# Norming the first eight heads while the last pair is computed, and starting the output projection with half sums of four tiles

## The chip, the cores and the metric

The kernel is one program on one core of a Trainium2 chip. Its engines are TensorE (PE: matrix products and transposes; "PEld" in a profile is its weight load), VectorE (DVE), ScalarE (ACT), GpSimd (POOL) and SyncE (SP, which here only issues transfers). Each engine works through its own list of instructions in order; semaphores order work between engines. The metric is the device time of one execution in microseconds; less is better.

## The reference, cut to what matters

Two transformer blocks run one after the other on 256 tokens of width 1024. The change lies in the second block, between its attention and the projection behind it. The sixteen heads are computed, the first eight (neighbourhood attention) and the last eight (dilated attention) are each normed over their own 512 features, and the two halves side by side go through one 1024 x 1024 projection:

```python
y = jnp.concatenate([rmsnorm(merge(o_na), out_norm_na_g[l]),
                     rmsnorm(merge(o_dil), out_norm_dil_g[l])], axis=-1) @ w_out[l]
x = x + g1 * y
h2 = rmsnorm(x, norm2_g[l]) * (1.0 + sc2) + sh2
```

`rmsnorm` divides by the root of the mean square over the features and multiplies by a gain. What comes behind (`h2`, its queries and the two large tables) is not touched.

## The kernel before

Activations are kept transposed: a tile is 128 features x 256 tokens. Sixteen heads are eight pairs, one tile `oT[:, n, :]` a pair; tiles 0 to 3 are the first eight heads, tiles 4 to 7 the last eight. Every float32 product is made of three fp32r products: each operand is split into a high part (`WH`, `YH`, written by ScalarE) and a low part (`WL`, `YL`, the difference, written by VectorE), and TensorE adds high x high, high x low and low x high. A tile of the output projection thus is 8 x 3 = 24 matmuls of 128x256, and its eight tiles are 192.

Weights come as a stream of chunks of 128x1024, one chunk an output tile, through a ring of four slots (`raw`, `WH`, `WL`). `hi(c)` on ScalarE makes the high part of chunk `c` once the tile of chunk `c - 4` is done (`chunk_done`); `lo(c)` on VectorE makes the low part once the high one is there (`h_done`), and TensorE waits for it (`l_done`). The chunks of the output projection are `C_COUT` to `C_COUT + 7`. Before the change the attention's steps prepare them up to `C_COUT + 2`; `C_COUT + 3` is prepared as the first thing of the projection's loop.

The attention is software-pipelined over steps m = 0 to 10 (`mix_step` on three engines). A step m < 8 projects the queries and keys of pair m; TensorE then computes the scores of pair m - 1 (L1608), the values product of pair m - 2 (`values`, L1630), the transposes of the probabilities of pair m - 1 (`turn_probs`, L1620) and of the output of pair m - 2 (`turn_out`, L1638). VectorE adds the bias and takes the maximum (`soft_in`: L971, L976, L982), divides the output by its sum (`o_out`, L1005, tile `on`) and, a step later, copies the transposed output to `oT` (L1107, semaphore `ot_done`). ScalarE computes the exponentials (`exps`, L510), copies the transposed probabilities (`pt_out`, tile `pT`, L520) and squares the `oT` tiles (L475); GpSimd adds the squares (L1411). So the last pair has its scores in step 8, its values in step 9, and its `oT` tile in step 10.

A norm is `spread(k)` on TensorE (a product with ones that sums the squares over partitions, L1530), then `rms(k)` on VectorE: the mean into `nm` (L808), a wait for `root(k)` on ScalarE (square root of `nm` into `nt`, L403), the reciprocal (L810) and one Newton step (L800 to L803) into `R`. Norm 4 is that of the first eight heads, norm 5 that of the last eight. Behind them `normed` multiplies `oT` by gain and `R` into `FY` (L1134, semaphore `yf_ready`), `norm_high` on ScalarE makes `YH` (L615) and `normed_low` on VectorE makes `YL` (L867, `yl_ready`). The order on VectorE behind the steps is written out:

```python
steps(dve, mix_step)
rms(4, D // 2, EPS_B, ps[:, 0, T:2 * T])
...
normed(0)
rms(5, D // 2, EPS_B, ps[:, 7, 0:T])
normed(1)
normed_low(0)
normed_low(1)
```

TensorE's projection, `out_steps`, waits once for all eight `YL` tiles and then does the eight output tiles one after the other in two alternating banks (L1495). VectorE adds each, scaled, to `x` (`cout_step`, L1150); ScalarE squares the new `x` for the next norm.

Of the kernel before, what the change touches and what calls it, by code (L numbers as in the profile page):

```python
# [16 lines left out]
T = 256  # L17
# [89 lines left out]
def two_block_kernel(nc, stream, xT, vecs, cI, cB, rows, wsT, adaT, att_bias, skT, spill, out):  # L107
    with ExitStack() as ctx:
# [267 lines left out]
        def _(act):  # L376
# [215 lines left out]
            def mix_step(m, g=None):  # L592
                if m < 8:
                    hi(C_QK + 2 * m + 3, g)
                    act.wait_ge(chunk_done, up(C_QK + 2 * m + 1, g, 4))
                    act.wait_ge(s_mm, up(8 + m - 1, g, 2))
                    act.activation(qs[:, m % 2, :], ps[:, m % 2, 0:T], ACT.Copy).then_inc(qt_ready, 1)
                    hi(C_QK + 2 * m + 4, g)
                if g is not None or m >= 3:
                    sq_tile(24 + m - 3, oT, ot_done, m - 2, m - 3, g, 2)  # L600
                if 1 <= m <= 8:
                    exps(8 + m - 1, g, False)
                if m < 8:
                    load_ada(41 + m, g)
                if 1 <= m <= 8:
                    pt_out(8 + m - 1, g)
                    if m < 8:
                        load_bias(m + 1, g)
# [8 lines left out]
            root(4)  # L617
# [7 lines left out]
            def cout_step(n, g=None):  # L625
                hi(C_COUT + 3 + n, g)
                if g is not None or n >= 1:
                    cout_square(n - 1, g)
# [147 lines left out]
        def _(dve):  # L776
# [324 lines left out]

            def mix_step(m, g=None):
                if m < 8:
                    lo(C_QK + 2 * m + 3, g)
                if g is not None or m >= 3:
                    dve.wait_ge(ot_mm, up(8 + m - 2, g, 2))
                    dve.tensor_copy(tiles(oT, m - 3, g, 2), ps[:, 2 + m % 2:3 + m % 2, T:2 * T]).then_inc(ot_done, 1)  # L1107
                if 1 <= m <= 8:
                    soft_in(8 + m - 1, g, False)
                if 2 <= m <= 9:  # L1110
                    o_out(8 + m - 2, g)
                if m < 8:
# [11 lines left out]
            rms(4, D // 2, EPS_B, ps[:, 0, T:2 * T])  # L1124
# [4 lines left out]
            dve.wait_ge(ot_done, NPAIR)  # L1129

            def normed(k):

                for n in range(4 * k, 4 * k + 4):
                    dve.scalar_tensor_tensor(out=FY[:, n, :], in0=oT[:, n, :], scalar=vec[:, V_OG + n:V_OG + n + 1],  # L1134
                                             in1=R[:, k, :], op0=ALU.mult, op1=ALU.mult).then_inc(yf_ready, 1)

            def normed_low(k):
                for n in range(4 * k, 4 * k + 4):
                    y_low(n, AG + 8 + n, FY[:, n:n + 1, :], None, 1)

            normed(0)
            rms(5, D // 2, EPS_B, ps[:, 7, 0:T])
            normed(1)
            normed_low(0)
            normed_low(1)

            def cout_step(n, g):
                lo(C_COUT + 3 + n, g)
                dve.wait_ge(chunk_done, up(C_COUT + n + 1, g, 4))
                dve.scalar_tensor_tensor(out=tiles(x, n, g, 4), in0=ps[:, n % 2:n % 2 + 1, 0:T],  # L1150
# [3 lines left out]
            with dve.Fori(0, 2) as g:  # L1154
                for n in range(4):
                    cout_step(n, g)

            dve.wait_ge(bias_in[0], (NPAIR // 2 + 1) * 16)
            dve.tensor_tensor(diags[:, :, :], ident.unsqueeze(1).broadcast_to([P, KC, P]),
                              mod[:, 40:48].unsqueeze(2).broadcast_to([P, KC, P]), ALU.mult).then_inc(diag_ready, 1)  # L1160

# [324 lines left out]
        def _(pe):  # L1486
# [214 lines left out]
            def mix_step(m, g=None):  # L1701
# [4 lines left out]
                if 1 <= m <= 8:  # L1706
# [4 lines left out]
                    scores(8 + p, g, p % 2)  # L1711
                if m >= 2:
# [17 lines left out]
                if m == 8:  # L1730
                    spread(4, sacc_done, 28, tmp[5][:, :], bank=0, at0=T)
# [3 lines left out]
            out_steps(C_COUT, AG + 16, 24)  # L1735
# [227 lines left out]
```

## Time and profile before

| what | us |
|---|---|
| median of 3 runs | 1441.45 (1438.92 to 1443.35) |
| the profiled execution: its time | 1439.84 |
| its span, first to last instruction | 1437.8 |
| TensorE busy | 1312.4 (91%) |
| VectorE busy | 1003.8 (70%) |
| ScalarE busy | 758.1 (53%) |
| GpSimd busy | 348.0 (24%) |
| mean granted TensorE clock | 0.956 of full |

The profile's times are microseconds from the start of the span. A granted clock of 1.00 is TensorE's upper level, 2.4 GHz, and 0.50 the lower, 1.2 GHz. A busy TensorE need not be at its peak; idle time of an engine that nothing waits for costs nothing.

### The profile page before, as it was taken

What the parts mean: (1) busy time and instruction counts of PE and PEld (TensorE: products, weight loads), DVE (VectorE), ACT (ScalarE), POOL (GpSimd) and SP (SyncE); (2) the same over time, 40 slices, a digit from 0 to 9 for tenths busy, and PEclk for the clock granted to TensorE, in tenths of its full rate; (3) what the DMA queues carried; (4) which work ended last, traced back from release to release, by engine and by line L of the source; (5) the groups of instructions that cost most, each with busy time, mean ns of one, the idle gap of its engine ahead of it and who ended that gap; (6) DMA issues with size and microseconds to landing.
All of it is one profiled execution on the core that took longest, in us unless ns stands there. A gap on an engine that the chain in (4) does not pass through costs nothing.

```text
span 1437.8 us, 26848 instructions
## 1 busy us (share of the span) xinstructions
PE 1312.4 (91%) x8582; PEld 1181.9 (82%) x8582; DVE 1003.8 (70%) x1875; ACT 758.1 (53%) x1259; POOL 348.0 (24%) x233
## 2 busy tenths in 40 slices
PE   5989998998399857999999999999999999999994
PEld 5979998887398846998999977777888888888883
DVE  7689987884647755788788855555666666666664
ACT  5444354554245534554888854444555555555553
POOL 0068812112200013778677710000000000000000
PEclk9989999997699968999999999999999999999998
DMA  7867785442246513555233345555565655655562
GB/s 287 326 226 253 260 261 165 147 149 77 100 162 216 179 45 126 163 165 188 91 107 114 118 134 179 180 179 172 181 193 183 192 188 187 191 181 192 182 194 97
DMA packets 67878, 249.18 MB, mean 173 GB/s; under 512 B 7792, under 2 KB 8176, under 8 KB 66928
## 3 DMA queue, kind: packets, MB, share of 16 engines
q1 hardware_dynamic: 59184, 216.89, 45.9%
q10 hardware_dynamic: 8640, 31.59, 6.5%
q8 instruction: 31, 0.51, 0.1%
q14 instruction: 23, 0.19, 0.0%
HBM read 245.83 MB, written 2.62 MB: 173 GB/s over the span
## 4 chain that ended last, share of the span: by engine, by line
PE 82%; DVE 10%; ACT 3%; issue 2%; DMA 1%; POOL 1%; DVEq 0%; ACTq 0%; SPq 0%; POOLq 0%
PE ps L1495 34%; PE ps L1823 25%; PE ps L1834 10%; PE ps L1836 5%; PE ps L1804 4%; ACT pr L510 2%; DVE s L971 1%; DVE small L976 1%; PE ps L1620 1%; PE ps L1608 1%; DVE R L810 1%; PE ps L1630 1%; DVE WL L785 1%; PE ps L1566 1%; DMA ada<-adaT 1%
## 5 line engine op out<-in xcount | busy, mean ns | idle before, releaser
L785 DVE TENSOR_TENSOR WL<-raw,WH 128x1024 fp32r<-128x1024 f32 x326 | 409.3, 1259 | 175.7 <-ACT WH L399 172.7
L399 ACT ACTIVATE WH<-raw 128x1024 fp32r<-128x1024 f32 x394 | 414.0, 1055 | 195.5 <-PE ps L1495 87.1
L1495 PE MATMUL ps<-X,WH 128*128 128x256 f32 x1872 | 351.9, 289 | 13.3 <-DVE X L1089 7.4
L1495 PEld LDWEIGHTS ps<-X,WH 128*128 128x128 f32 x1872 | 295.8, 195 | 15.1 <-DVE X L1089 8.2
L1495 PE MATMUL ps<-X,WL 128*128 128x256 f32 x936 | 267.4, 286 | 0.0
L1834 PE MATMUL ps<-X,WH 128*128 128x512 f32 x608 | 216.9, 397 | 0.0
L1823 PE MATMUL ps<-WH,wvH 128*128 128x512 f32 x512 | 205.6, 402 | 2.5 <-DVE wvL L1289 2.1
L1823 PE MATMUL ps<-WH,wvL 128*128 128x512 f32 x512 | 202.6, 396 | 0.0
L1823 PE MATMUL ps<-WL,wvH 128*128 128x512 f32 x512 | 202.3, 395 | 0.0
L1464 POOL TENSOR_TENSOR WL<-raw,WH 128x1024 fp32r<-128x1024 f32 x68 | 164.4, 2420 | 82.9 <-ACT WH L399 82.8
L1495 PEld LDWEIGHTS ps<-X,WL 128*128 128x128 f32 x936 | 181.6, 194 | 0.0
L1836 PE MATMUL ps<-X,WL 128*128 128x256 f32 x608 | 170.5, 280 | 0.0
L1834 PEld LDWEIGHTS ps<-X,WH 128*128 128x128 f32 x608 | 114.2, 188 | 27.6
L1823 PEld LDWEIGHTS ps<-WH,wvH 128*128 128x128 f32 x512 | 96.9, 189 | 39.4 <-DVE wvL L1289 15.6
L1836 PEld LDWEIGHTS ps<-X,WL 128*128 128x128 f32 x608 | 114.7, 189 | 2.9
L1823 PEld LDWEIGHTS ps<-WH,wvL 128*128 128x128 f32 x512 | 96.6, 189 | 22.4
L1823 PEld LDWEIGHTS ps<-WL,wvH 128*128 128x128 f32 x512 | 96.7, 189 | 17.4
L1495 PE MATMUL ps<-WH,X 128*128 128x256 f32 (+1 forms) x416 | 79.5, 292 | 24.3 <-DVE X L1089 19.4
L1495 PE MATMUL ps<-YH,WH 128*128 128x256 f32 x256 | 73.9, 289 | 17.4 <-DVE YL L867 17.4
L1495 PEld LDWEIGHTS ps<-WH,X 128*128 128x128 f32 x416 | 68.3, 201 | 25.9 <-issue 24.6
L740 ACT ACTIVATE tmp<-tmp 128x256 f32<-128x256 f32 x76 | 31.7, 418 | 107.7 <-DVE tmp L1298 107.7
L1495 PE MATMUL ps<-YL,WH 128*128 128x256 f32 x256 | 73.4, 287 | 0.0
(233 smaller groups left out, 2070.1 us busy)
## 6 DMA issues: line engine op xcount, KB each, us to landing
raw<-stream SPq DMA_DIRECT2D x394, 512.0 KB, 3.4
ada<-adaT ACTq DMA_DIRECT2D x48, 512.0 KB, 3.6
bias<-att_bias ACTq DMA_DIRECT2D x9, 512.0 KB, 4.6
x<-xT SPq DMA_DIRECT2D x1, 1024.0 KB, 4.7
ws<-wsT SPq DMA_DIRECT2D x1, 1024.0 KB, 7.1
lng<-rows SPq DMA_DIRECT2D x1, 1024.0 KB, 8.0
lnb<-rows SPq DMA_DIRECT2D x1, 1024.0 KB, 7.6
bsb<-rows SPq DMA_DIRECT2D x1, 1024.0 KB, 7.6
```

What stands on the lines that cost most here:

```text
L399: act.activation(WH[:, slot, :], raw[:, slot, :], ACT.Copy).then_inc(h_done, 1)
L510: act.activation(pr[:, k, :], s[:, k, :], ACT.Exp, bias=negm[:, k:k + 1], accum_out=small_den[:, par, k:k + 1]).then_inc(p_ready, 1)
L740: act.activation(tmp[i % 2][:, :], tmp[i % 2][:, :], ACT.Gelu).then_inc(gelu_ready, 1)
L785: dve.tensor_tensor(WL[:, slot, :], raw[:, slot, :], WH[:, slot, :].bitcast(F32), ALU.subtract).then_inc(l_done, 1)
L810: link(dve.reciprocal(R[:, k % 2, :], nt[:, :]))
L971: ins = dve.scalar_tensor_tensor(out=s[:, :, :].rearrange("p (h t) k -> p h (t k)", h=2), in0=ps[:, 4:6, :], scalar=HD ** -0.5, in1=b, op0 ...
L1464: pool.tensor_tensor(WL[:, slot, :], raw[:, slot, :], WH[:, slot, :].bitcast(F32), ALU.subtract).then_inc(l_done, 1)
L1495: mm = pe.matmul(out_ap, a(kc), b(kc), start=(first and kc == 0 and i == 0), stop=(last and kc == KC - 1 and i == 2))
L1804: mm = pe.matmul(ps[:, gate_bank(e) + half, k * P:(k + 1) * P], O1[:, n, :], (O2a, O2b[:, e % 2])[half][:, k, :], start=True, stop=True)
L1823: mm = pe.matmul(ps[:, 4 + 2 * t + h, :], a[:, j % 2, ts_], b[:, slot, hs], start=(first and i == 0), stop=(last and i == 2), skip_group_c ...
L1834: pe.matmul(ps[:, i % 2, :].rearrange("p (x t) -> p x t", x=2), wh(kc), X1[:, :, kc, :], start=(kc == 0), stop=False, skip_group_check=True)
L1836: mm = pe.matmul(ps[:, i % 2, 0:T], wl(kc), X1H[:, kc, :], start=False, stop=(kc == KC - 1), skip_group_check=True)
```

## The change

Five things are rearranged; no arithmetic is changed.

- Norm 4 moves into the steps. TensorE's `spread(4)` stands ahead of the values product of step 8, VectorE writes `nm` in step 8 behind `o_out`, ScalarE takes the root in step 8 between the exponentials and the copies of the transposed probabilities, and VectorE does the reciprocal, the Newton step and the first two `normed` tiles in step 9, one ahead of and one behind `o_out`.
- `hi` and `lo` of chunk `C_COUT + 3` move into step 8, at its start.
- Behind the steps VectorE does the other two tiles of the first half and their four `YL`, then norm 5, then `normed` and `normed_low` of the second half interleaved.
- TensorE takes four output tiles in four banks at once: for each the 12 matmuls of the first half of the features, and then for each the 12 of the second half. It waits for `YL` tile by tile. The last four output tiles are done as before, in the same four banks.
- The small sums on `mod` move behind the norm, and `diags` moves ahead of the last four `cout_step`.

```diff
@@ ScalarE
                     act.activation(qs[:, m % 2, :], ps[:, m % 2, 0:T], ACT.Copy).then_inc(qt_ready, 1)
                     hi(C_QK + 2 * m + 4, g)
+                if m == 8:
+                    hi(C_COUT + 3)
                 if g is not None or m >= 3:
                     sq_tile(24 + m - 3, oT, ot_done, m - 2, m - 3, g, 2)
                 if 1 <= m <= 8:
                     exps(8 + m - 1, g, False)
+                if m == 8:
+                    root(4)
...
-            root(4)
             norm_high(0)
             root(5)
             norm_high(1)
...
             def cout_step(n, g=None):
-                hi(C_COUT + 3 + n, g)
                 if g is not None or n >= 1:
+                    hi(C_COUT + 3 + n, g)
                     cout_square(n - 1, g)
@@ VectorE
+            def normed(n):
+
+                dve.scalar_tensor_tensor(out=FY[:, n, :], in0=oT[:, n, :], scalar=vec[:, V_OG + n:V_OG + n + 1],
+                                         in1=R[:, n // 4, :], op0=ALU.mult, op1=ALU.mult).then_inc(yf_ready, 1)
+
+            def normed_low(n):
+                y_low(n, AG + 8 + n, FY[:, n:n + 1, :], None, 1)
+
             def mix_step(m, g=None):
                 if m < 8:
                     lo(C_QK + 2 * m + 3, g)
+                if m == 8:
+                    lo(C_COUT + 3)
                 if g is not None or m >= 3:
                     dve.wait_ge(ot_mm, up(8 + m - 2, g, 2))
                     dve.tensor_copy(tiles(oT, m - 3, g, 2), ps[:, 2 + m % 2:3 + m % 2, T:2 * T]).then_inc(ot_done, 1)
                 if 1 <= m <= 8:
                     soft_in(8 + m - 1, g, False)
+                if m == 9:
+                    dve.wait_ge(root_ready, 5)
+                    link(dve.reciprocal(R[:, 0, :], nt[:, :]))
+                    newton(R[:, 0, :], nm[:, :], nt[:, :], r_ready)
+                    dve.wait_ge(r_ready, 5)
+                    dve.wait_ge(ot_done, 4)
+                    normed(0)
                 if 2 <= m <= 9:
                     o_out(8 + m - 2, g)
+                if m == 8:
+                    dve.wait_ge(psn_ready, 5)
+                    dve.tensor_scalar(nm[:, :], ps[:, 0, T:2 * T], 2.0 / D, EPS_B, ALU.mult, ALU.add).then_inc(m_ready, 1)
+                if m == 9:
+                    normed(1)
...
             steps(dve, mix_step)
-            rms(4, D // 2, EPS_B, ps[:, 0, T:2 * T])
+            normed(2)
+            normed(3)
+            for n in range(4):
+                normed_low(n)
+            rms(5, D // 2, EPS_B, ps[:, 7, 0:T])
+            dve.wait_ge(ot_done, NPAIR)
+            for n in range(4, 8):
+                normed(n)
+                if n >= 5:
+                    normed_low(n - 1)
+            normed_low(7)
...
-                dve.scalar_tensor_tensor(out=tiles(x, n, g, 4), in0=ps[:, n % 2:n % 2 + 1, 0:T],
+                dve.scalar_tensor_tensor(out=tiles(x, n, g, 4), in0=ps[:, n:n + 1, 0:T],
@@ TensorE
                     scores(8 + p, g, p % 2)
+                if m == 8:
+                    spread(4, sacc_done, 28, tmp[5][:, :], bank=0, at0=T)
...
-                if m == 8:
-                    spread(4, sacc_done, 28, tmp[5][:, :], bank=0, at0=T)
 
             steps(pe, mix_step)
             spread(5, sacc_done, 32, qb[:, 0, :])
-            out_steps(C_COUT, AG + 16, 24)
+
+            def cout_half(n, k0):
+
+                pe.wait_ge(l_done, C_COUT + n + 1)
+                wh, wl = weight(WH, (C_COUT + n) % RING), weight(WL, (C_COUT + n) % RING)
+                for kc in range(k0, k0 + 4):
+                    if n == 0:
+                        pe.wait_ge(yl_ready, AG + 8 + kc + 1)
+                    yh, yl = YH[:, kc, :], YL[:, kc, :]
+                    for i, (a, b) in enumerate(((wh, yh), (wh, yl), (wl, yh))):
+                        mm = pe.matmul(ps[:, n, 0:T], a(kc), b, start=(kc == 0 and i == 0), stop=(kc == KC - 1 and i == 2))
+                return mm
+
+            pe.wait_ge(m_ready, 5)
+            for n in range(4):
+                if n == 2:
+                    pe.wait_ge(ot_done, NPAIR)
+                cout_half(n, 0)
+            for n in range(4):
+                cout_half(n, 4).then_inc(chunk_done, 1)
+            with pe.Fori(1, 2) as g:
+                for n in range(4):
+                    pe.wait_ge(x_ready, up(20 + n + 1, g, 4))
+                    feature_tile(C_COUT + n, g, n, YH, YL)
             spread(6, sacc_done, 40, tmp[5][:, :])
```

What the program's lists of instructions show of this, at three places. First VectorE from the start of step 8 (behind the steps' loop), before; the first five rows are step 8:

```order
L1107 COPY oT<-ps 128x256
L971 SCALAR_TENSOR_TENSOR s<-ps,bias 128x1024
L976 TENSOR_REDUCE small<-s 128x4
L982 TENSOR_SCALAR small<-small 128x4
L1005 TENSOR_TENSOR on<-ps,small 128x256
L996 RECIPROCAL small<-small 128x4
L1107 COPY oT<-ps 128x256
L1005 TENSOR_TENSOR on<-ps,small 128x256
L1107 COPY oT<-ps 128x256
L808 TENSOR_SCALAR nm<-ps 128x256
L810 RECIPROCAL R<-nt 128x256
```

The same engine and place in the changed kernel (L788 is `lo`, L1120 the copy to `oT`, L974 to L985 `soft_in`):

```order
L788 TENSOR_TENSOR WL<-raw,WH 128x1024
L1120 COPY oT<-ps 128x256
L974 SCALAR_TENSOR_TENSOR s<-ps,bias 128x1024
L979 TENSOR_REDUCE small<-s 128x4
L985 TENSOR_SCALAR small<-small 128x4
L1008 TENSOR_TENSOR on<-ps,small 128x256
L1134 TENSOR_SCALAR nm<-ps 128x256
L999 RECIPROCAL small<-small 128x4
L1120 COPY oT<-ps 128x256
L1125 RECIPROCAL R<-nt 128x256
L803 TENSOR_TENSOR nt<-R 128x256
```

The low part of a chunk now stands ahead of the last pair's `soft_in`, and the reciprocal of norm 4 two rows behind the last exponentials' sum instead of behind the last `oT`.

Second ScalarE from step 8 on; the lines with + and - are of one piece of the difference:

```order
+L399 ACTIVATE WH<-raw 128x1024
 L475 ACTIVATE tmp<-oT 128x256
 L510 ACTIVATE pr,small<-s,small 128x256 x4
-L520 ACTIVATE pT<-ps 128x512 x2
-L475 ACTIVATE tmp<-oT 128x256 x2
 L403 ACT_TABLE_LOAD
 L403 ACTIVATE nt<-nm 128x256
-L615 ACTIVATE YH<-FY 128x256 x4
+L520 ACTIVATE pT<-ps 128x512 x2
+L475 ACTIVATE tmp<-oT 128x256 x2
+L619 ACTIVATE YH<-FY 128x256 x4
```

The high part of the chunk stands ahead of the square and the exponentials, and the one table load and the square root ahead of the copies to `pT`.

Third TensorE behind the steps' loop, before and then in the changed kernel (L1550 is `spread`, L1628 the scores, L1650 the values, L1640 and L1658 the transposes):

```order
L1608 MATMUL ps<-ks,qs 128x256 x4
L1630 MATMUL ps<-vC,pT 128x64 x8
L1620 MATMUL ps<-idio,pr 128x128 x8
L1638 MATMUL ps<-idio,on 128x128 x2
L1530 MATMUL ps<-tmp,ones 128x256
L1630 MATMUL ps<-vC,pT 128x64 x8
L1638 MATMUL ps<-idio,on 128x128 x2
L1530 MATMUL ps<-qb,ones 128x256
```

```order
L1550 MATMUL ps<-tmp,ones 128x256
L1650 MATMUL ps<-vC,pT 128x64 x8
L1640 MATMUL ps<-idio,pr 128x128 x8
L1658 MATMUL ps<-idio,on 128x128 x2
L1650 MATMUL ps<-vC,pT 128x64 x8
L1658 MATMUL ps<-idio,on 128x128 x2
L1550 MATMUL ps<-qb,ones 128x256
```

`spread(4)`, the product on `tmp`, moved from behind the last pair's transposes to ahead of the values of the pair before it; behind `spread(5)` the projection starts in both.

## Rows read from the trace of the kernel before

**Rows 1.** Waits of TensorE, 490 to 580 us: total, times, longest.

```profile
PE ps L1495 <- DVE YL L867: 14.4, 1, 14.4
PE ps L1495 <- DVE X L1089: 7.4, 1, 7.4
```

**Rows 2.** Chain that ended last, in order of time: start, us, what.

```profile
508.83 0.43 DVE oT L1107
...
524.82 1.10 DVE YL L867 x3
...
526.25 24.47 PE ps L1495 x192
```

**Rows 3.** Timeline of VectorE, 487 to 522 us: start, us, instruction, idle before.

```profile
487.04 1.23 DVE L785 TENSOR_TENSOR WL<-raw,WH 128x1024 fp32r<-128x1024 f32 x1 [1.44 <-ACT WH L399]
488.18 0.42 DVE L1107 COPY oT<-ps 128x256 f32 x1
...
496.53 1.23 DVE L971 SCALAR_TENSOR_TENSOR s<-ps,bias 128x1024 f32<-128x1024 f32 x1 [0.17 <-PE ps L1608]
...
507.62 0.42 DVE L1005 TENSOR_TENSOR on<-ps,small 128x256 f32<-128x256 f32 x1 [4.06 <-PE ps L1630]
...
511.46 1.75 DVE L810 RECIPROCAL R<-nt 128x256 f32<-128x256 f32 x1 [1.88 <-ACT nt L403]
...
514.49 0.43 DVE L803 TENSOR_TENSOR R<-R,nt 128x256 f32<-128x256 f32 x1
...
517.16 0.42 DVE L808 TENSOR_SCALAR nm<-ps 128x256 f32<-128x256 f32 x1
...
521.56 1.67 DVE L1134 SCALAR_TENSOR_TENSOR FY<-oT,vec,R 128x256 f32<-128x256 f32 x4
```

**Rows 4.** Timeline of ScalarE, 485 to 524 us.

```profile
485.47 0.59 ACT L520 ACTIVATE pT<-ps 128x512 f32<-128x512 f32 x1
485.94 1.06 ACT L399 ACTIVATE WH<-raw 128x1024 fp32r<-128x1024 f32 x1
...
495.71 0.59 ACT L520 ACTIVATE pT<-ps 128x512 f32<-128x512 f32 x1
...
501.14 0.19 ACT L510 ACTIVATION_READ_ACCUMULATOR pr<-s,small 128x1 f32 x1
502.71 1.09 ACT L520 ACTIVATE pT<-ps 128x512 f32<-128x512 f32 x2 [1.38 <-PE ps L1620]
...
509.72 1.28 ACT L403 ACT_TABLE_LOAD   x1
511.01 0.42 ACT L403 ACTIVATE nt<-nm 128x256 f32<-128x256 f32 x1
...
522.07 1.60 ACT L615 ACTIVATE YH<-FY 128x256 fp32r<-128x256 f32 x4 [4.05 <-DVE FY L1134]
```

**Rows 5.** Timeline of TensorE, 501 to 530 us.

```profile
501.38 1.29 PE L1620 MATMUL ps<-idio,pr 128*128 128x128 f32 x8 [2.96 <-ACT pr L510]
...
503.94 3.65 PE L1630 MATMUL ps<-vC,pT 128*128 128x64 f32 x16
...
510.64 1.22 PE L1530 MATMUL ps<-qb,ones 128*128 128x256 f32 x2 [1.85 <-POOL qb L1411]
526.25 0.58 PE L1495 MATMUL ps<-YH,WH 128*128 128x256 f32 x1 [14.39 <-DVE YL L867]
...
529.40 0.31 PE L1495 MATMUL ps<-YH,WL 128*128 128x256 f32 x1
```

**Rows 6.** Windows: us, busy us of each engine (instructions), PEclk, DMA share, GB/s.

```profile
499.00:500.00 1.00, 0.00 (x0) 0.00 (x0) 0.61 (x3) 0.75 (x3) 0.00 (x0) 1.00 0.12 49
...
504.00:505.00 1.00, 1.00 (x5) 1.00 (x6) 0.00 (x0) 0.10 (x1) 0.72 (x1) 0.50 0.00 0
```

**Rows 7.** Timeline of TensorE, first block's attention: transposes of probabilities and output.

```profile
332.05 1.97 PE L1620 MATMUL ps<-idio,pr 128*128 128x128 f32 x8 [1.69 <-ACT pr L510]
333.81 0.63 PE L1638 MATMUL ps<-idio,on 128*128 128x128 f32 x2
```

More of the change, by code:

```diff
@@ L1128, in _, with cout_step @@
             link(dve.tensor_tensor(s2, s2, vec[:, V_N2:V_N2 + 8], ALU.mult))
[L1129 to L1148, printed above, removed]
+            def cout_step(n, g=None):
+                if g is not None or n >= 1:
+                    lo(C_COUT + 3 + n, g)
                 dve.wait_ge(chunk_done, up(C_COUT + n + 1, g, 4))
-                dve.scalar_tensor_tensor(out=tiles(x, n, g, 4), in0=ps[:, n % 2:n % 2 + 1, 0:T],
+                dve.scalar_tensor_tensor(out=tiles(x, n, g, 4), in0=ps[:, n:n + 1, 0:T],
                                          scalar=column(mod[:, 16:24], n, g, 4), in1=tiles(x, n, g, 4),
                                          op0=ALU.mult, op1=ALU.add).then_inc(x_ready, 1)
-            with dve.Fori(0, 2) as g:
-                for n in range(4):
-                    cout_step(n, g)
+            for n in range(4):
+                cout_step(n)
             dve.wait_ge(bias_in[0], (NPAIR // 2 + 1) * 16)
@@ L1160, in _ @@
                               mod[:, 40:48].unsqueeze(2).broadcast_to([P, KC, P]), ALU.mult).then_inc(diag_ready, 1)
+            with dve.Fori(1, 2) as g:
+                for n in range(4):
+                    cout_step(n, g)
             rms(6, D, EPS_B, ps[:, 7, 0:T])
@@ L1729, in mix_step @@
                     turn_out(8 + m - 2, g)
-                if m == 8:
-                    spread(4, sacc_done, 28, tmp[5][:, :], bank=0, at0=T)
             steps(pe, mix_step)
             spread(5, sacc_done, 32, qb[:, 0, :])
-            out_steps(C_COUT, AG + 16, 24)
+            def cout_half(n, k0):
[13 more added lines that the diff above has]
+                cout_half(n, 0)
+            for n in range(4):
+                cout_half(n, 4).then_inc(chunk_done, 1)
+            with pe.Fori(1, 2) as g:
+                for n in range(4):
+                    pe.wait_ge(x_ready, up(20 + n + 1, g, 4))
+                    feature_tile(C_COUT + n, g, n, YH, YL)
             spread(6, sacc_done, 40, tmp[5][:, :])
```

## The prediction

> **What bounds the kernel now.** I read the page first: TensorE is busy 91% of the span and holds most of the chain that ended last, so time is to be won only where TensorE stands idle and something else finishes the chain. Next I asked who TensorE waits for around the changed code. One wait stands out [rows 1]: 14.4 us in front of the second block's output projection, put down to the last `YL` tile. The 7.4 us wait behind the projection, for `X`, is not touched by the change. The chain in order of time [rows 2] shows what fills the first wait. The last pair's output is copied to `oT` at 508.83, and the projection's 192 matmuls start at 526.25, 17.42 us later, and take 24.47 us, to 550.72. Between them lie, in sequence on VectorE and ScalarE, two complete norms and sixteen split tiles. Four of the eight pairs were there long before. So the question is what part of the 17.42 us still lies between the last `oT` and the first matmul, and whether what is moved ahead of that `oT` makes it late.
>
> The timelines of VectorE, ScalarE and TensorE [rows 3 to 5] give the durations and, between two starts, the pitch. I write the new times on the scale of the old span; up to 496 us nothing differs.
>
> **Step 8: the chunk moved ahead of the last softmax.** Before, `soft_in` of the last pair starts at 496.53, as soon as its scores are there (idle 0.17, put down to TensorE) [rows 3]. Now `lo(C_COUT + 3)` is queued ahead of it on VectorE, and needs `hi(C_COUT + 3)`, which ScalarE can start only behind the copies to `pT`. The second of them starts at 495.71, and the pitch from such a copy to `WH` is 485.94 - 485.47 = 0.47 [rows 4], so `hi` runs from 496.18 to 497.24. `lo` follows 0.04 later, as 487.04 follows 485.94 + 1.06 [rows 3, 4]; the copy to `oT` follows 1.14 behind (488.18 - 487.04), at 498.42, and `soft_in` some 0.38 behind that (a copy lasts 0.42), at 498.80. The last softmax is **2.27 us late**. Queued behind the waiting `lo` are that `oT` copy, `soft_in` and `o_out`, and TensorE waits for all of them; there is no cover. The moved `hi` itself is covered: ScalarE would have been waiting for the exponentials' input.
>
> **Step 8: the root ahead of the probabilities' copies.** The exponentials ended at 501.33 [rows 4], now at 503.60, and TensorE's transposes start 2.27 later, at 503.65. They took 1.29, partly at the upper clock. In the window from 499 to 500 TensorE was idle at a granted clock of 1.00, and from 504 to 505 it had 0.50 [rows 6]. The idle stretch ahead of the transposes was 2.96 us [rows 5] and grows to about 4.7, so I take all eight at the lower level: 1.97, as the same eight in the first block at 332.05 [rows 7]. They end at 505.62. Meanwhile ScalarE does the table load and the root, 1.28 + 0.42, to 505.30 [rows 4]: hidden behind the transposes, with 0.3 us to spare. Copies to `pT` run from 505.66 to 506.75 (1.09), and the last values product starts at 506.80 against 503.94. It takes 3.65, as before [rows 5], to 510.45. `spread(4)` is gone from in front of it, but it had been hidden behind the copies (502.71 + 1.09 = 503.80), which is worth 0.1. At its new place it is free as well: TensorE then has nothing to do before the late transposes.
>
> **Step 9: the reciprocal ahead of `o_out`.** The output transposes of the pair before start some 0.2 ahead of 505.62 and take 0.63 [rows 7], to 506.04. VectorE copies `oT` at 506.08, starts the reciprocal at 506.42, and has `R` 3.46 later (511.46 to 514.49 + 0.43) [rows 3], at 509.88; `normed(0)` runs to about 510.34. `o_out` is wanted at 510.47: no delay, but only 0.1 us to spare. From `o_out` to the `oT` copy it is 1.21 (507.62 to 508.83), so the last `oT` comes at 511.68 in place of 508.83. **In all it is 2.85 us late.**
>
> **From the last `oT` to the projection.** Square, add and `spread(5)` stay: it started 1.81 behind `oT` (508.83 to 510.64) and took 1.22 [rows 3, 5]; now 513.49 to 514.71. In that time VectorE does `normed(2)` and `normed(3)`, at a pitch of 0.40 (1.67 for four, less overlap), until 512.8. ScalarE has the square to 512.6 and makes `YH` at a pitch of 0.40 (four in 1.60 [rows 4]), and VectorE's `YL` follows each: the first is there at 513.4, the fourth at 514.6. So TensorE can start right behind `spread(5)`, at **514.75 in place of 526.25**. The 17.42 us between have become 3.07.
>
> **The second half while the first runs.** Norm 5 starts at 514.75; from its `nm` to `normed` it was 4.40 (517.16 to 521.56) [rows 3], so `normed(4)` starts at 519.15, and with the interleaved order `YL` 4 is there at 520.5 and `YL` 7 at about 522.4 (eight instructions of 0.40, the first `YL` 0.1 behind its `YH`). TensorE has 48 matmuls before it needs them. Before, the first fourteen took from 526.25 to 529.40, 0.225 each, at the lower clock, and the other 178 the remaining 21.32, 0.12 each [rows 2, 5]. With that profile the 48 last 3.15 + 34 x 0.12 = 7.2, to 522.0, and the quarter of `YL` 7 is wanted at 523.0. No stall, 0.6 us to spare.
>
> **Weights behind it.** The output tile of a first chunk now ends at 523.4, behind 36 matmuls of other tiles that the old order had later; only then can `hi(C_COUT + 4)` start, and `lo` ends 1.06 + 1.23 [rows 3, 4] later, at 525.7. TensorE wants it at 514.75 + 96 matmuls, 527.7. The next chunks follow at 1.43 a tile of second halves against 2.9 us a tile of use, so the margin of 2.0 us grows. `diags` (one 128x1024 instruction, 1.23 by the nearest row, `lo`) lies in that margin. The small sums on `mod` lie behind the last `YL`, and their first user is later. The 192 matmuls so run through in 24.47 us, to 539.22 against 550.72, and behind that nothing changes its order.
>
> **The sum.** -17.42 + 3.07 + 2.85 = **-11.5 us**. Against the profiled execution, 1439.84, that is 1428.3; the median of three is 1.6 higher and scatters over 4.4, and on its scale it is 1430.0. I say 1429.5, nearer to the median.
>
> **The unknown costs and their bounds.** The late softmax is between 0 (if `lo` costs no wait) and 2.3. The matmuls at the lower clock are between none of the first fourteen (14 x 0.105 = 1.5 less) and all 48 of the first halves (34 x 0.105 = 3.6 more). I take the same fourteen, as TensorE again comes from little work (7 us after the last big product). The table load between two kinds of work was seen only behind a square, where it took 1.28; a second one's length on top is the upper bound. Together: 1429.5 - 1.5 - 2.3 = 1425.7 and 1429.5 + 3.6 + 0.9 = 1434.0.
>
> **Rivals.**
> - *The table load costs more where it stands now.* ScalarE's root is ready at 505.30 for copies at 505.66. If the load holds ScalarE for another 1.28, the root ends at 506.58, the copies are 0.93 late, and so is all behind them: -10.6, 1430.4. Against it: in the old place the root started at 511.01, the moment the load ended [rows 4]. Chance 0.06. The Trainium skill (ScalarE: Activation LUTs, "What ACT_TABLE_LOAD costs") gives about 1.28 us for the load and about 1.38 us for a drain, 2.66 in all for each switch of set; the trace agrees with the load and shows no drain behind it, though there the engine had just one instruction ahead of the load. By the page the sum would be about 1 us less gain.
> - *The first halves stay slow, or stall.* All 48 at the lower clock end at about 525.6: 3.6 us of the gain gone, 1433.1. For it: TensorE had half the clock all the way through the values product, though busy 3.65 us [rows 5, 6]. Against it: the same kind of matmul got the full clock 3.15 us after the start [rows 5]. Chance 0.10.
> - *The gain is larger*, 1426 to 1427: full clock with the first matmuls, or a softmax less late. The bound rows speak against it. Chance 0.04.
> - *The change doesn't do what it says.* The wait only moves: TensorE starts early but stands before the second halves or the fifth tile until VectorE and ScalarE have done what they did before. For it speak margins of 0.6 and 2.0 us; against it, that even a stall of 2 us leaves 9.5. To fall within 4.3 us of no change it has to lose 7.2 of the 11.5. Chance 0.04.
> - *Slower.* One mechanism does it: the granted clock. If the projection, with its new stops for `YL` one by one, stayed at 0.50 throughout, its other 178 matmuls would cost 0.105 more each, 18.7 us, which leaves the kernel 7.2 us slower, 1448.6 on the median's scale. It decides from 11.5 / 0.105 = 110 more slow matmuls, over half the projection. Against it: the half-speed stretch before lasted fourteen. Chance 0.03.
>
> **How the numbers follow.** The forecast of -11.5 has 0.73, the rivals 0.06, 0.10, 0.04, 0.04 and 0.03. About 0.3% (4.3 us) can be told from no change. All cases but the last two are faster by more: faster 0.93, same 0.04, slower 0.03. The range goes from 1425.5 to 1434.5, the bounds above with half a us for the scatter of the runs, and leaves out mainly the last two rivals.
>
> **What would show it.** In the changed kernel: `soft_in` of the last pair at 498.8, idle before it for `lo`, itself for `WH`; transposes at the lower clock; the root ending before the transposes do; the reciprocal ended before the values product; the last `oT` near 511.7; the projection's first matmul right behind `spread(5)`, near 514.8, no wait inside it, and 24 to 25 us from its first to its last. The prediction is wrong if the wait for `YL` inside the projection is more than 1 us, if the clock comes back later than 4 us after the start, or if the last `oT` is later than 513.

## The result and the profile after

The changed kernel took **1429.89 us** (median of 4 runs, 1429.45 to 1430.42) against 1442.01 (4 runs, 1438.92 to 1443.35): a ratio of 0.9923, 95% interval 0.9908 to 0.9937. It is 12 us (0.8%) faster; 1429.5 had been predicted, in a range of 1425.5 to 1434.5.

The waits of TensorE come first, now from 485 to 570 us; columns as in [rows 1].

```profile
PE ps L1515 <- DVE X L1092: 6.7, 1, 6.7
PE ps L1640 <- ACT pr L510: 5.3, 3, 4.8
PE ps L1550 <- POOL tmp L1431: 1.9, 1, 1.9
PE ps L1550 <- POOL qb L1431: 1.9, 1, 1.9
PE ps L1650 <- ACT pT L520: 0.8, 1, 0.8
```

The wait of 14.4 us for `YL` [rows 1] is gone. The wait for the last exponentials (`pr`) is longer, 4.8 against 2.96 [rows 5]: that is the late softmax. No row for `YL` is left, so the half sums never stood. The wait for `X` behind the projection reads 6.7 in place of 7.4, but nothing is won there: from the norm's mean to the first matmul of the queries it is 12.50 us against 12.49 (543.18 to 555.68, and 554.24 to 566.73). TensorE's own products between the two took 0.7 longer, since the granted clock was at 0.50 to 547 us, some 3 us, and in the kernel before for some 2; they end before `X` is there.

The timeline of VectorE:

```profile
488.00 1.23 DVE L788 TENSOR_TENSOR WL<-raw,WH 128x1024 fp32r<-128x1024 f32 x1 [1.44 <-ACT WH L399]
...
498.25 1.23 DVE L788 TENSOR_TENSOR WL<-raw,WH 128x1024 fp32r<-128x1024 f32 x1 [1.38 <-ACT WH L399]
499.39 0.42 DVE L1120 COPY oT<-ps 128x256 f32<-128x256 f32 x1
499.73 1.22 DVE L974 SCALAR_TENSOR_TENSOR s<-ps,bias 128x1024 f32<-128x1024 f32 x1
...
510.82 0.48 DVE L1107 SCALAR_TENSOR_TENSOR FY<-oT,vec,R 128x256 f32<-128x256 f32 x1
511.48 0.42 DVE L1008 TENSOR_TENSOR on<-ps,small 128x256 f32<-128x256 f32 x1 [0.17 <-PE ps L1650]
...
512.69 0.42 DVE L1120 COPY oT<-ps 128x256 f32<-128x256 f32 x1 [0.39 <-PE ps L1658]
...
515.79 0.42 DVE L811 TENSOR_SCALAR nm<-ps 128x256 f32<-128x256 f32 x1
...
520.20 0.88 DVE L1107 SCALAR_TENSOR_TENSOR FY<-oT,vec,R 128x256 f32<-128x256 f32 x2
521.17 0.43 DVE L870 TENSOR_TENSOR YL<-FY,YH 128x256 fp32r<-128x256 f32 x1
...
522.64 0.99 DVE L870 TENSOR_TENSOR YL<-FY,YH 128x256 fp32r<-128x256 f32 x2
...
526.07 1.23 DVE L788 TENSOR_TENSOR WL<-raw,WH 128x1024 fp32r<-128x1024 f32 x1 [0.60 <-ACT WH L399]
```

The first row answers to 487.04 in [rows 3]; everything here is 0.96 later for reasons ahead of the change, so I measure from that row on. `lo` at 498.25 waits for `WH`, and `soft_in` follows it without any idle time of its own: 11.73 behind the first row, against 9.49. `o_out` at 511.48 had to wait 0.17 for the values, so the reciprocal and `normed(0)` ahead of it came just in time.

ScalarE in step 8:

```profile
497.16 1.06 ACT L399 ACTIVATE WH<-raw 128x1024 fp32r<-128x1024 f32 x1
...
504.32 0.19 ACT L510 ACTIVATION_READ_ACCUMULATOR pr<-s,small 128x1 f32 x1
504.53 1.28 ACT L403 ACT_TABLE_LOAD   x1
505.82 0.42 ACT L403 ACTIVATE nt<-nm 128x256 f32<-128x256 f32 x1
506.57 1.08 ACT L520 ACTIVATE pT<-ps 128x512 f32<-128x512 f32 x2 [0.33 <-PE ps L1640]
```

The load starts 0.02 us behind the last exponential's read-out, the root 0.01 behind the load, and the copies to `pT` still wait 0.33 for TensorE: table load and root are hidden.

TensorE's timeline, and the chain over the same time:

```profile
504.56 1.97 PE L1640 MATMUL ps<-idio,pr 128*128 128x128 f32 x8 [4.76 <-ACT pr L510]
506.32 0.63 PE L1658 MATMUL ps<-idio,on 128*128 128x128 f32 x2
507.80 3.65 PE L1650 MATMUL ps<-vC,pT 128*128 128x64 f32 x16 [0.84 <-ACT pT L520]
...
515.77 0.41 PE L1765 MATMUL ps<-YL,WH 128*128 128x256 f32 x1
...
519.82 0.41 PE L1765 MATMUL ps<-YH,WL 128*128 128x256 f32 x1
520.03 0.33 PE L1765 MATMUL ps<-YH,WH 128*128 128x256 f32 x1
520.20 0.28 PE L1765 MATMUL ps<-YL,WH 128*128 128x256 f32 x1
```

```profile
514.54 1.22 PE ps L1550 x2
515.75 13.39 PE ps L1765 x96
529.15 11.40 PE ps L1515 x96
```

`spread(5)` and the 192 matmuls follow each other without a gap. 21 of them ran at the lower clock, to 520.03, where the kernel before had 14 [rows 5].

For comparisons I use **the changed stretch**: from the start of that first row (the first of the two `lo` in step 7, in every kernel) to the first matmul of the queries behind the projection. It was 79.69 us before and is 67.68 now, 12.01 less. Marks within it, in us from its start (the kernels below the second row are the experiments; "slow" counts the projection's matmuls at the lower clock; where the projection's first matmul begins under `spread(5)`, without a wait, the start given is that of its second):

| kernel | last `oT` | projection starts | last `x` | stretch | slow |
|---|---|---|---|---|---|
| before | 21.79 | 39.21 | 63.85 | 79.69 | 14 |
| changed | 24.69 | 27.75 | 52.58 | 67.68 | 21 |
| after_again | 24.68 | 27.75 | 52.61 | 67.71 | 22 |
| lo_late | 22.02 | 25.09 | 49.92 | 65.02 | 19 |
| no_halves | 24.68 | 35.67 | 60.68 | 75.78 | 17 |
| halves_alone | 20.63 | 35.50 | 60.19 | 75.94 | 15 |
| diags_back | 24.68 | 27.75 | 52.74 | 68.22 | 21 |
| root_late | 26.51 | 29.57 | 53.82 | 68.92 | 14 |
| root_again | 26.51 | 29.58 | 53.84 | 69.19 | 13 |
| warm | 21.10 | 23.61 | 48.32 | 63.42 | 0 |
| warm_split | 20.20 | 23.16 | 48.14 | 63.24 | 0 |
| warm_nm | 20.20 | 23.15 | 47.56 | 63.09 | 0 |

### The profile page after: what moved, and what is told of

The parts are those of the page before. It is cut to its first block, busy times and chain, and to the rows that moved or that the text cites. A ratio compares the mean times of both kernels' runs of the same rounds, so it can differ in the third digit from the quotient of the medians.

```text
span 1427.7 us, 26814 instructions
## 1 busy us (share of the span) xinstructions
PE 1315.0 (92%) x8582; PEld 1185.4 (83%) x8582; DVE 1004.6 (70%) x1875; ACT 758.1 (53%) x1259; POOL 345.8 (24%) x233
## 4 chain that ended last, share of the span: by engine, by line
PE 82%; DVE 9%; ACT 3%; issue 2%; DMA 2%; POOL 1%; DVEq 0%; ACTq 0%; SPq 0%; POOLq 0%
PE ps L1515 32%; PE ps L1866 25%; PE ps L1877 10%; PE ps L1879 5%; PE ps L1847 4%; ACT pr L510 2%; DVE small L979 1%; DVE s L974 1%; PE ps L1640 1%; DMA ada<-adaT 1%; PE ps L1765 1%; PE ps L1628 1%; PE ps L1650 1%; DVE WL L788 1%; PE ps L1586 1%
## 5 line engine op out<-in xcount | busy, mean ns | idle before, releaser
L788 DVE TENSOR_TENSOR WL<-raw,WH 128x1024 fp32r<-128x1024 f32 x326 | 409.8, 1261 | 174.2 <-ACT WH L399 171.4
L1326 DVE TENSOR_TENSOR tmp<-tmp,A 128x256 f32<-128x256 f32 x76 | 32.4, 426 | 51.9 <-ACT tmp L743 51.9
L1515 PE MATMUL ps<-YH,WH 128*128 128x256 f32 x224 | 64.4, 287 | 3.0 <-DVE YL L870 3.0
```

The source lines that it names most:

```text
L788: dve.tensor_tensor(WL[:, slot, :], raw[:, slot, :], WH[:, slot, :].bitcast(F32), ALU.subtract).then_inc(l_done, 1)
L1326: dve.tensor_tensor(tmp[2 + i % 2][:, :].unsqueeze(1), tmp[i % 2][:, :].unsqueeze(1), tiles(A, EARLY + i, g, 2), ALU.mult).then_inc(w_read ...
L1515: mm = pe.matmul(out_ap, a(kc), b(kc), start=(first and kc == 0 and i == 0), stop=(last and kc == KC - 1 and i == 2))
```

## The experiments

**after_again** is the changed kernel unaltered, beside root_again on the same chip.

> The changed kernel once more, unaltered, to see how far its total and the length of the changed stretch come back. From the start of the second-last lo of the steps to the first matmul of the queries behind the projection it took 67.68 us, and 79.69 in the kernel before. If that stretch is what the change moves and the rest only scatters: 67.7 to 68.3 here, with a total of 1428 to 1431.

Measured: stretch 67.71 against 67.68. Total 1427.39 (1425.76 to 1428.90), 2.5 us below the first set and below the 1428 to 1431 that I expected. But the kernel before, run beside it, was 2.5 lower too (1439.51 against 1442.01), so the difference of the medians is 12.12 us in both sets. The ratio is 0.9914 (0.9901 to 0.9928), which overlaps with 0.9923 (0.9908 to 0.9937). So a total can be set only against the kernel before of its own set, and even then the interval of a ratio is about 2 us wide to either side. The stretch of this kernel comes back to 0.03 us; where variants differ by less than the totals can tell, the stretch is what I read.

**lo_late** takes one suspected cost away.

```diff
@@ VectorE, mix_step
-                if m == 8:
-                    lo(C_COUT + 3)
...
                     dve.tensor_scalar(nm[:, :], ps[:, 0, T:2 * T], 2.0 / D, EPS_B, ALU.mult, ALU.add).then_inc(m_ready, 1)
+                    lo(C_COUT + 3)
```

> The changed kernel, with lo of chunk C_COUT+3 moved in step 8 from ahead of the oT copy and soft_in to behind nm; hi stays. Theory 1 (the moved chunk makes the last softmax 2.3 us late and nothing hides it): soft_in follows its scores at once, the values product starts 2.6 us earlier than in the changed kernel, the reciprocal still ends before it, and all behind moves with it: 2.6 us faster than the changed kernel, about 1427.3. Theory 2 (the reciprocal or the slow transposes would hold the chain anyway): the softmax is earlier but the last oT is not, 1429.9.

Measured: 1425.64 (1422.74 to 1426.98), ratio 0.9894 (0.9877 to 0.9910); stretch 65.02, 2.66 less than in the changed kernel. The rows of VectorE:

```profile
496.99 1.23 DVE L974 SCALAR_TENSOR_TENSOR s<-ps,bias 128x1024 f32<-128x1024 f32 x1 [0.16 <-PE ps L1627]
...
500.38 1.22 DVE L788 TENSOR_TENSOR WL<-raw,WH 128x1024 fp32r<-128x1024 f32 x1
```

`soft_in` waits for its scores again and not for the chunk, and `lo` lies in the time in which the exponentials run. The last `oT` is 2.67 earlier, and so is all behind it. Theory 1 holds: the place of `lo` cost the change 2.7 us. The total is 14.7 below the kernel before of its set (1440.38), 2.6 more than the change's 12.1; but the ratios' intervals overlap, so the proof is the stretch.

**no_halves** and **halves_alone** take the two parts of the change apart. The first keeps all but the half sums:

```diff
@@ TensorE
-            pe.wait_ge(m_ready, 5)
-            for n in range(4):
-                if n == 2:
-                    pe.wait_ge(ot_done, NPAIR)
-                cout_half(n, 0)
-            for n in range(4):
-                cout_half(n, 4).then_inc(chunk_done, 1)
+            pe.wait_ge(yl_ready, AG + 16)
+            for n in range(4):
+                feature_tile(C_COUT + n, None, n, YH, YL)
```

> The changed kernel, but the first four output tiles are done whole, one after the other, behind a wait for all eight YL. Theory 1 (of the gain about 8 us come from starting on the first half while norm 5 runs, the rest from norm 4 in the steps): the first matmul starts about 8 us later than in the changed kernel, right behind the last YL, and about 0.7 us come back as fewer matmuls run at the lower clock: 1437, still 5 us faster than the kernel before. Theory 2 (the half sums bring little, since their matmuls would stall for the second half): within 2 us of the changed kernel.

The second adds to the kernel before only `cout_half`, its calls and the four banks:

> The kernel before, with only TensorE's half sums (and the four banks) of the change: both norms stand behind the last pair as before. Theory 1: the first matmul can start at the first YL instead of the last, 2.7 us earlier; nothing stalls: 1439.3. The two parts then don't add up to the change (2.7 and 5 against 12): each needs the other. Theory 2 (half sums bring the gain by themselves): below 1435.

Measured: no_halves 1436.93 (1432.39 to 1440.24), ratio 0.9978 (0.9966 to 0.9989), stretch 75.78, that is 3.91 less than before and 8.10 more than in the changed kernel. halves_alone 1437.76 (1434.02 to 1442.38), ratio 0.9984 (0.9971 to 0.9996), stretch 75.94, 3.75 less than before; of this about 1.1 is not the half sums' but the clock's, as its last values product took 2.59 instead of 3.65 us. The granted clock rose within that product, from 0.50 in the window from 507 to 508 us to 1.00 from 509 to 510; in the kernel before it stayed at 0.50 through the same sixteen matmuls:

```profile
507.05 2.59 PE L1630 MATMUL ps<-vC,pT 128*128 128x64 f32 x16
...
525.51 0.55 PE L1744 MATMUL ps<-YH,WH 128*128 128x256 f32 x1 [11.85 <-DVE YL L867]
```

The parts give 3.9 and 3.75, together 7.7, and the whole gives 12.0. (Of the 3.9, 0.74 lie behind the last `x`; they belong to `diags` and the clock, see the next experiment.) The 4.3 beyond (5.4 without the clock's part) are there only together: the half sums can run under norm 5 only if norm 4 and the first four `YL` are done before it.

**diags_back** moves one instruction back.

```diff
@@ VectorE
             for n in range(4):
                 cout_step(n)
-            dve.wait_ge(bias_in[0], (NPAIR // 2 + 1) * 16)
-            dve.tensor_tensor(diags[:, :, :], ident.unsqueeze(1).broadcast_to([P, KC, P]),
-                              mod[:, 40:48].unsqueeze(2).broadcast_to([P, KC, P]), ALU.mult).then_inc(diag_ready, 1)
             with dve.Fori(1, 2) as g:
                 for n in range(4):
                     cout_step(n, g)
+            dve.wait_ge(bias_in[0], (NPAIR // 2 + 1) * 16)
+            dve.tensor_tensor(diags[:, :, :], ident.unsqueeze(1).broadcast_to([P, KC, P]),
+                              mod[:, 40:48].unsqueeze(2).broadcast_to([P, KC, P]), ALU.mult).then_inc(diag_ready, 1)
```

> The changed kernel, with diags moved back behind the last cout_step. In the changed kernel the time from the projection's last matmul to the mean of the next norm is 2.6 us against 3.5 in the kernel before. Theory 1 (diags beside GpSimd's last add slows that add from 0.72 to 1.10, and TensorE's spread then is later and partly slow): back at its old place the add takes about 1.1 again and the stretch 3.0 to 3.5 us, 0.4 to 0.9 us slower than the changed kernel. Theory 2 (the stretch is shorter by the clock's chance alone): add and stretch stay as in the changed kernel.

Measured: 1430.28 (1426.01 to 1431.91), ratio 0.9920 (0.9902 to 0.9937); stretch 68.22, 0.54 more. VectorE and GpSimd at the end of the projection, then TensorE's `spread(6)`:

```profile
541.97 0.48 DVE L1169 SCALAR_TENSOR_TENSOR x<-ps,small,x 128x256 f32<-128x256 f32 x1 [0.51 <-PE ps L1516]
542.37 1.22 DVE L1180 TENSOR_TENSOR diags<-idio,small 128x1024 f32<-128x1024 f32 x1
```

```profile
543.06 1.10 POOL L1432 TENSOR_TENSOR tmp<-tmp 128x256 f32<-128x256 f32 x1 [1.01 <-ACT tmp L475]
```

```profile
544.22 0.70 PE L1551 MATMUL ps<-tmp,ones 128*128 128x256 f32 x2 [2.29 <-POOL tmp L1432]
```

In the changed kernel the same add takes 0.72, and the same spread 0.70; from the last `x` on VectorE to the mean of the next norm it is 2.60, and 2.98 with `diags` back:

```profile
540.58 0.48 DVE L1169 SCALAR_TENSOR_TENSOR x<-ps,small,x 128x256 f32<-128x256 f32 x1 [0.48 <-PE ps L1515]
543.18 0.43 DVE L811 TENSOR_SCALAR nm<-ps 128x256 f32<-128x256 f32 x1 [2.12 <-PE ps L1550]
```

```profile
541.67 0.72 POOL L1431 TENSOR_TENSOR tmp<-tmp 128x256 f32<-128x256 f32 x1 [0.98 <-ACT tmp L475]
```

In the kernel before they took 1.10 and 1.06, and the whole 3.35:

```profile
550.89 0.48 DVE L1150 SCALAR_TENSOR_TENSOR x<-ps,small,x 128x256 f32 x1 [0.61 <-PE ps L1495]
554.24 0.42 DVE L808 TENSOR_SCALAR nm<-ps 128x256 f32<-128x256 f32 x1 [1.73 <-PE ps L1530]
```

```profile
551.98 1.10 POOL L1411 TENSOR_TENSOR tmp<-tmp 128x256 f32<-128x256 f32 x1 [1.11 <-ACT tmp L475]
```

```profile
553.14 1.06 PE L1530 MATMUL ps<-tmp,ones 128*128 128x256 f32 x2 [2.43 <-POOL tmp L1411]
```

So both theories have a part. The add beside `diags` costs 0.38 and is undone by the move; the spread's 0.36 is the clock, which the experiment left at its upper level (granted 1.00 from 543 to 545 us, against 0.67 from 553 to 554 in the kernel before). The place of `diags` alone doesn't settle the clock: at its old place the spread took 1.06, 0.98 (halves_alone) and 0.70 (diags_back); moved, it took 0.70 in seven kernels, but 0.95 in root_again and 1.14 in warm_nm. Whether it has a part in it stays open. The remaining 0.16 of the 0.54 arose before the last `x`. The totals can't tell this kernel from the changed one.

**root_late** moves the root, and the table load with it, behind the copies.

```diff
@@ ScalarE, mix_step
-                if m == 8:
-                    root(4)
...
                     pt_out(8 + m - 1, g)
...
+                if m == 8:
+                    root(4)
```

> The changed kernel, with the root of norm 4 (and its table load) on ScalarE behind the copies to pT of step 8 instead of ahead of them. In the changed kernel the root ends 0.33 us before the transposes do, and the reciprocal chain lets o_out go 0.2 us after its input. Theory 1 (the load costs 1.28 and hides where it stands; the margin of step 9 is thin): the copies to pT start no earlier, the root ends about 3.4 us later against the copies, the reciprocal then ends about 1.7 us behind the values product and o_out waits for it: 1.7 us slower than the changed kernel, 1431.6. Theory 2 (the load holds ScalarE longer than its 1.28 us, on the path): the copies come earlier and the kernel is faster, 1429 or less.

Measured: 1427.55 (1427.25 to 1430.27), ratio 0.9919 (0.9905 to 0.9932). The median, 2.3 below the changed kernel's, looked like Theory 2, but the stretch is 68.92, 1.24 longer. On VectorE:

```profile
506.99 1.75 DVE L1125 RECIPROCAL R<-nt 128x256 f32<-128x256 f32 x1 [1.99 <-ACT nt L403]
...
510.48 0.48 DVE L1107 SCALAR_TENSOR_TENSOR FY<-oT,vec,R 128x256 f32<-128x256 f32 x1
510.89 0.42 DVE L1008 TENSOR_TENSOR on<-ps,small 128x256 f32<-128x256 f32 x1
```

The reciprocal waits for the root, `o_out` has no wait of its own left, and TensorE's wait for `on` grew from 0.5 to 2.3. The last `oT` is 1.82 later; 0.6 came back because only 14 projection matmuls were slow. The median seemed to say the opposite, so I repeated it beside the changed kernel.

> The kernel root_late once more, on the same chip as the changed kernel. It had the lower total (1427.55 against 1429.89) and the longer changed stretch (68.92 against 67.68). Theory 1 (the stretch tells, the total of one set of runs doesn't): stretch 68.5 to 69.5 again, and a total 0 to 2 us above that of the changed kernel beside it. Theory 2 (the root behind the copies is better by something outside the stretch): again 2 us below it.

Measured: 1428.42 (1427.36 to 1434.18) against 1427.39 beside it, ratio 0.9931 (0.9915 to 0.9947); stretch 69.19. Theory 1 holds. The lower median of the first set was no gain of this kernel: the kernel before was 2.3 lower in that set too (1439.67 against 1442.01), and against it root_late won 12.12 us, exactly as much as the changed kernel. The stretch came back to 0.27 here, of which 0.25 is a slower `spread(6)` (0.95 against 0.70).

**warm** asks what the lower clock costs. It is lo_late with matmuls that fill TensorE's waits.

```diff
@@ TensorE
+            def keep_warm(n):
+                for _ in range(n):
+                    pe.matmul(ps[:, 1, T:2 * T], X1H[:, 0, 0:P], X1H[:, 1, :], start=True, stop=True)
...
                     values(8 + p, g, v_of)
+                if m == 8:
+                    keep_warm(18)
...
                     turn_out(8 + m - 2, g)
+                if m == 8:
+                    keep_warm(10)
+                if m == 9:
+                    keep_warm(14)
```

> The kernel lo_late with 42 matmuls added whose result nothing reads (128x256, into an unused half of a bank): 18 behind the values product of step 8, 10 behind the output transposes of step 8, 14 behind those of step 9, in stretches in which TensorE waited. Theory 1 (the lower clock is a price of those waits, on the path): the granted clock stays at 1.00 from the last softmax into the projection, the last values product takes 2.0 instead of 3.65 us, but o_out then waits for normed(0) and gets 0.9 of the 1.7; spread(5) and the first 21 projection matmuls save 0.6 and 2.0; the second halves stall 0.9 us for their YL: 2.9 us faster than lo_late, about 1422.7. Theory 2 (VectorE and ScalarE set the time and TensorE's clock is hidden): within 1 us of lo_late, 1425.6.

Measured: 1421.57 (1419.43 to 1423.53), ratio 0.9877 (0.9861 to 0.9893); stretch 63.42, 1.60 less than lo_late: more than the 1 of Theory 2 and not the 2.9 of Theory 1. The last values product took 1.97, and every one-microsecond window from the last softmax into the projection had a granted clock of 1.00. TensorE and its waits from 498 to 532 us:

```profile
500.80 1.97 PE L1649 MATMUL ps<-vC,pT 128*128 128x64 f32 x16 [0.30 <-ACT pT L520]
...
512.72 0.28 PE L1774 MATMUL ps<-YH,WL 128*128 128x256 f32 x1
513.69 0.36 PE L1774 MATMUL ps<-YH,WH 128*128 128x256 f32 x1 [0.70 <-DVE YL L870]
```

```profile
PE ps L1657 <- DVE on L1008: 1.5, 1, 1.5
PE ps L1774 <- DVE YL L870: 0.7, 1, 0.7
```

The projection starts 1.48 earlier than in lo_late, but is hardly shorter: 24.7 from start to last `x` against 24.8. Its first halves are done before the second half's `YL` are there, and each of the next four groups of three matmuls then has to wait for its own tile. With TensorE at its upper clock, norm 5 on VectorE and ScalarE is the bound there. Ahead of it the norm of step 9 holds `o_out`: TensorE waits 1.5 for `on`, against 0.5 in the changed kernel.

**warm_split** and **warm_nm** follow that up. The first puts `o_out` of step 9 ahead of the last two instructions of the Newton step, and `normed(0)` and `normed(1)` behind the last `oT` copy:

> The kernel warm, with o_out of step 9 ahead of the last two instructions of the Newton step of norm 4 and normed(0) and normed(1) behind the last oT copy. Theory 1 (in warm, VectorE's norm of step 9 holds o_out): o_out starts right behind the values product, 0.8 us earlier than in warm, and the last oT with it; 0.5 to 0.8 us faster than warm. Theory 2 (the second halves' YL set the end in any case, or the first YL come too late now): within 0.3 us of warm.

The second also puts the mean of norm 5 ahead of three of the four `YL`:

```diff
@@ VectorE
-            for n in range(4):
-                normed_low(n)
-            rms(5, D // 2, EPS_B, ps[:, 7, 0:T])
+            normed_low(0)
+            dve.wait_ge(psn_ready, 6)
+            dve.tensor_scalar(nm[:, :], ps[:, 7, 0:T], 2.0 / D, EPS_B, ALU.mult, ALU.add).then_inc(m_ready, 1)
+            for n in range(1, 4):
+                normed_low(n)
+            dve.wait_ge(root_ready, 6)
+            link(dve.reciprocal(R[:, 1, :], nt[:, :]))
+            newton(R[:, 1, :], nm[:, :], nt[:, :], r_ready)
+            dve.wait_ge(r_ready, 6)
```

> The kernel warm_split, with the mean of norm 5 on VectorE behind the first YL instead of behind all four. In warm_split the last oT came 0.9 us earlier than in warm but nm only 0.17, and the projection stood 1.2 us for the second half's YL. Theory 1 (at the full clock it is norm 5 on VectorE that sets the end): nm is 1.0 us earlier, the reciprocal 0.4 to 0.5 (it waits for the fourth YL now), and the stretch is 0.4 to 0.5 shorter than 63.24. Theory 2 (TensorE or the weights set it): 63.2.

Measured: warm_split 1422.43 (1417.81 to 1425.88), ratio 0.9874 (0.9853 to 0.9895); last `oT` 0.90 earlier than in warm, stretch only 0.18 shorter: Theory 2, because VectorE still has four `FY` and four `YL` ahead of `nm`. warm_nm 1424.09 (1421.01 to 1424.69), ratio 0.9885 (0.9869 to 0.9901); last `x` 0.58 earlier than in warm_split, as its reciprocal is, but the stretch only 0.15 shorter, since `spread(6)` took 1.14 instead of 0.70 this time. So norm 5 is confirmed as the bound up to the last `x`, and the end of the stretch doesn't show it. The totals of the three can't be told apart. The ratios of warm and warm_split lie below both intervals of the changed kernel; those of warm_nm and of lo_late, which has no added matmuls, reach into them, and there only the stretch, 4.6 and 2.7 shorter than the changed kernel's, shows the gain.

## Why the prediction was right, point by point

**What bounded the kernel** was read rightly: the 14.4 us wait was on the path, and the time behind the projection stayed as it was, but for the last point below.

**Step 8, the late softmax.** Predicted 2.27 late, measured 11.73 - 9.49 = 2.24. lo_late shows that it is the place of `lo` alone.

**Step 8, root and transposes.** Predicted: the root ends 0.3 ahead of the transposes, which take 1.97 at the lower clock. Measured: it ends at 506.24 and they at 506.53, 0.29 later, and they take 1.97. The rival that the table load costs more was wrong. The Trainium skill (ScalarE: Activation LUTs, "What ACT_TABLE_LOAD costs") gives a drain of about 1.38 us besides the load's 1.28. No run here shows one, neither behind the four exponentials (504.53 to 505.82) nor behind the copies in root_late, where the load ran at 505.25 and the root at 506.54.

**Step 9, the reciprocal ahead of `o_out`.** Predicted margin 0.1, measured 0.17. root_late shows what lies behind it: a root 3.1 us later in the stretch made the reciprocal 2.1 and the last `oT` 1.8 later. The last `oT` was predicted 2.85 late and is 2.90 late.

**From the last `oT` to the projection.** Predicted 3.07, measured 515.75 - 512.69 = 3.06. With the term before, the start is 39.21 - 27.75 = 11.46 earlier; 11.5 was predicted.

**The second half under the first.** `YL` 4 was there at 521.60 and `YL` 7 at 523.63, and no wait arose. The quarter that needs `YL` 7 began at 524.36, a margin of 0.7 where I gave 0.6. That this fits is luck: seven more slow matmuls than I reckoned with made TensorE need it 0.65 later. In root_late, where 14 were slow as predicted, `YL` 7 was written from 522.60 on and the quarter began 0.06 behind its end:

```profile
522.60 0.42 DVE L870 TENSOR_TENSOR YL<-FY,YH 128x256 fp32r<-128x256 f32 x1
```

```profile
523.08 0.39 PE L1765 MATMUL ps<-YH,WH 128*128 128x256 f32 x1
```

So with the count that the prediction took, the margin is nothing: the first matmul had begun under the spread, so that the quarter was wanted some 0.4 earlier than reckoned, and the `YL` came some 0.2 later. In warm, where none were slow, TensorE did wait.

**The matmuls at the lower clock** were mis-sized: 14 predicted, 21 measured. Seven more at (519.82 - 515.77) / 19 = 0.213 in place of 0.12 are 0.65 us, which my term left out. From start to last `x` only 0.19 of it shows (24.83 against 24.64), mostly since the start in the chain, 515.75, is that of the second matmul: the first had begun under the spread. In the kernels of this study that left the waits unfilled the count was 13 to 22, with like work ahead of it, so it can't be forecast closer from these rows. The reason that I gave for fourteen, that the projection starts 7 us after the last big product, doesn't come out either: by the prediction's own times the values product ended at 510.45, 4.3 before the start. And one of the signs by which I called the prediction wrong came true: the clock was to come back within 4 us, and came back at 520.03, 4.8 after the first matmul at 515.19. What followed from it was small, but this term was taken by likeness and not worked out.

**Weights.** `lo(C_COUT + 4)` ended at 527.30, TensorE wanted it at 529.15: 1.85 against 2.0 predicted.

**What the sum left out** is the end: from the last `x` to the next norm's mean it is 0.75 shorter, 543.18 - 540.58 = 2.60 against 3.35. I costed `diags` at nothing where it was moved to and did not ask what it had cost where it was. 0.38 is the slower add beside it (diags_back), 0.36 the spread at the lower clock, which this time fell to the kernel before. The sum in the stretch is -11.3 to the last `x` and -12.0 with this; the medians differ by 12.1. That 1429.5 lies within 0.4 of the median is in part luck: the kernel before came out at 1442.01 and not at 1441.45, and its sets of runs differ by 2.5.

**The slower rival**, the whole projection at half clock, did not happen: 21 slow matmuls are far from the 110 more from which it decided.

## What to carry to other kernels

When work is moved ahead of a late result, ask for each moved instruction what it waits for and what is queued behind it: here the big move gained 14.4 us and one small weight split gave 2.7 of it back, though VectorE stood idle for 1.35 us a few instructions further on. Two changes that open and fill the same gap have to be made together, and measured apart they look small (3.9 and 3.75 of 12.0). And never set the total of one set of runs against that of another: the same kernel differed by 2.5 us between sets, and the kernel before by as much. For small differences compare a stretch between two fixed marks in the trace: it came back to 0.03 us for one kernel and 0.27 for another, and it showed a loss of 1.2 that the medians hid.

## What the runs showed of the hardware

A GpSimd add of 128x256 took 0.72 us with VectorE idle and 1.10 where it began under a VectorE product of two SBUF tiles of 128x1024 that had 0.5 us left. The Trainium skill (SBUF — State Buffer, "SBUF: two separate sides") says that such an operation and a GpSimd operation that reads SBUF take a shared port pair in turns, the second waiting for the first to end. The rows fit this roughly: 0.38 more for 0.53 of overlap, in the kernel before as in diags_back.

In the kernel before and the changed one the granted clock stayed at 0.50 through a values product of 3.65 us without a gap, and came back during the projection, behind 14 and 21 matmuls. In halves_alone it rose within the same values product, which then took 2.59. With the waits filled (warm) it stayed at 1.00 throughout; that was worth 1.6 us of the stretch, as VectorE's norm took over the rest.
